# Scaling of attention probabilities on ScalarE instead of VectorE in a two-block transformer kernel on one core

## The reference, cut to what matters

```python
s = jnp.einsum('nibkgd,nijkd->nikgbj', qb, kb).astype(jnp.float32) * (dh ** -0.5) + bias
s = jnp.where(mask[None, :, None, None], s, NEG_INF)
m = jnp.max(s, axis=-1)
if sink is not None:
    sk = sink.astype(jnp.float32).reshape(Hk, G)[:, :, None]
    m = jnp.maximum(m, sk)
p = jnp.exp(s - m[..., None])
denom = jnp.sum(p, axis=-1)
if sink is not None:
    denom = denom + jnp.exp(sk - m)
p = p / denom[..., None]
o = jnp.einsum('nikgbj,nijkd->nibkgd', p.astype(v.dtype), vb)
```

## Time and profile before

| | us |
|---|---|
| three timed runs, median | 3052.56 |
| lowest and highest of them | 3052.38, 3054.38 |
| the profiled execution's own time | 3057.37 |
| its span, first to last instruction | 3055.6 |
| PE busy in the span | 2493.0 (82%) |
| DVE busy | 1438.0 (47%) |
| ACT busy | 862.8 (28%) |
| POOL busy | 686.3 (22%) |
| bytes read from HBM | 1094 MB, 359 GB/s over the span |

### The profile page before, as it was taken

One profiled execution on the slowest core, in us unless ns is written; L12 is line 12 of the kernel. 1 busy time (PEld: TensorE's weight loads), 2 busy tenths in 40 slices (PEclk: granted clock), 3 DMA queues, 4 the chain that ended last, 5 costly groups with the idle time before them and its releaser, 6 DMA issues.

```text
span 3055.6 us, 32772 instructions
## 1 busy us (share of the span) xinstructions
PE 2493.0 (82%) x11448; PEld 1318.3 (43%) x11448; DVE 1438.0 (47%) x3379; ACT 862.8 (28%) x2297; POOL 686.3 (22%) x638
## 2 busy tenths in 40 slices
PE   8999865667999966657898987798987989877777
PEld 7777311113977421213555532264542645422222
DVE  3363100002255201000467667778657786677774
ACT  0231100000122100000233333457434574343343
POOL 4010000002211000000013444424334243444442
PEclk9999978778999987887899999999999999999999
DMA  6337999999434899999716999999999999999997
GB/s 260 137 133 305 424 428 428 428 428 384 166 138 181 371 426 428 427 427 427 310 46 274 422 421 421 421 421 421 415 422 421 416 393 417 420 421 422 421 419 312
DMA packets 121205, 1100.41 MB, mean 360 GB/s; under 512 B 13488, under 2 KB 17360, under 8 KB 21968
## 3 DMA queue, kind: packets, MB, share of 16 engines
q1 hardware_dynamic: 45584, 558.26, 43.9%
q0 software_dynamic: 73728, 536.90, 42.4%
q10 hardware_dynamic: 1728, 3.14, 0.3%
HBM read 1094.06 MB, written 4.19 MB: 359 GB/s over the span
## 4 chain that ended last, share of the span: by engine, by line
DMA 44%; PE 42%; DVE 8%; issue 3%; ACT 3%; POOL 1%; DVEq 0%; SPq 0%; ACTq 0%; POOLq 0%
DMA wbuf<-in_puv,ar 20%; PE ps L711 18%; PE ps L1431 9%; DMA wbuf<-in_w_expert_up 8%; DMA wbuf<-in_w_expert_down 8%; DMA wbuf<-in_w_expert_gate 5%; PE ps L901 4%; PE ps L1080 3%; DVE ar L2240 3%; DMA wbuf<-in_w_mem_kv 2%; PE ps L866 2%; PE ps L715 2%; ACT ar L2303 1%; PE ps L811 1%; PE ps L834 1%
## 5 line engine op out<-in xcount | busy, mean ns | idle before, releaser
L1431 PE MATMUL ps<-wbuf,ar 128*128 128x512 f32 x2048 | 969.4, 612 | 214.8 <-ACT ar L2303 214.4
L2240 DVE CUSTOM_DVE_ANT_0 ar<-wbuf,Y 128x1024 f32<-128x1024 f32 x512 | 628.4, 1227 | 334.5 <-DMA wbuf<-in_puv,ar 325.0
L2862 POOL DMA_INDIRECT wbuf<-in_puv,ar x512 | 554.3, 1083 | 863.7 <-PE ps L1431 745.6
L1431 PEld LDWEIGHTS ps<-wbuf,ar 128*128 128x128 f32 x2048 | 370.0, 193 | 765.1 <-issue 763.2
L1080 PE MATMUL ps<-wbuf,ar 128*32 128x512 f32 x2944 | 458.8, 760 | 284.1 <-DMA wbuf<-in_w_expert_up 113.0
L2303 ACT ACTIVATE ar<-ar 128x1 f32<-128x1 f32 (+1 forms) x1053 | 270.4, 257 | 667.3 <-DVE ar L2240 635.4
L711 PE MATMUL ps<-HT,wbuf 128*128 128x256 f32 (+1 forms) x2304 | 396.7, 331 | 4.9 <-DMA wbuf<-in_w_mem_kv 4.9
L711 PEld LDWEIGHTS ps<-HT,wbuf 128*128 128x128 f32 x2304 | 350.2, 193 | 50.6 <-issue 10.8
L1080 PEld LDWEIGHTS ps<-wbuf,ar 128*32 128x32 f32 x2944 | 93.1, 125 | 632.5 <-issue 212.7
L2300 ACT COPY ar<-ps 128x512 f32<-128x512 f32 (+4 forms) x135 | 70.1, 519 | 700.8 <-PE ps L1080 297.3
L2828 POOL TENSOR_TENSOR sm<-sm,co 128x1 f32<-128x1 f32 (+1 forms) x18 | 10.1, 561 | 1094.6 <-DVE sm L1466 1094.3
(11 more groups left out here) (188 smaller groups left out, 1954.1 us busy)
## 6 DMA issues: line engine op xcount, KB each, us to landing
wbuf<-in_w_expert_down SPq DMA_DIRECT2D x64, 2048.0 KB, 31.3
wbuf<-in_w_expert_up SPq DMA_DIRECT2D x62, 2048.0 KB, 30.9
wbuf<-in_w_expert_gate SPq DMA_DIRECT2D x58, 2048.0 KB, 30.8
wbuf<-in_w_in SPq DMA_DIRECT2D x22, 2048.0 KB, 9.5
wbuf<-in_peer_w_q SPq DMA_DIRECT2D x12, 2048.0 KB, 11.5
wbuf<-in_w_o SPq DMA_DIRECT2D x6, 2048.0 KB, 11.6
wbuf<-in_b_w_in SPq DMA_DIRECT2D x6, 2048.0 KB, 11.4
wbuf<-in_w_branch_b SPq DMA_DIRECT2D x4, 2048.0 KB, 7.5
```

The source lines that it names most:

```text
L1431: m = T.e.matmul(acc[n][:, :], DG[:, j % 4, :], rows_of(name)[:, 1024 + 512 * n:1536 + 512 * n], start=(j == 0), stop=(j == 127))
L2240: V.did(V.e.tensor_tensor_reduce(JK, rows_of(f"g{l}{i}.{j}")[:, 0:1024], Y[:, i, :], 1.0, 0.0, ALU.mult, ALU.add, DT[:, i, j:j + 1]), f"do ...
L2862: G.land(G.e.indirect_dma_start(out=rows_of(name), out_offset=None, in_=I["puv"], in_offset=bass.IndirectOffsetOnAxis(ap=IX[:, i, j:j + 1] ...
```

## The change

Three edits, all in `attend`. On VectorE the copy of the sink columns goes, and for units with a `scale` so does the multiplication; the reciprocal gets a name (`.rc`) so that ScalarE can wait for it. On ScalarE the copy of the sink columns comes ahead of the exponentials of its unit, and after the exponentials of unit k the tile of unit k-1 is multiplied by its reciprocals, as an activation `Copy` with a scale for each partition: one of 128x512 for a dilated unit, two of 128x256 for a windowed one. The other attentions keep their multiplication on VectorE.

```diff
@@ -1575,8 +1575,6 @@
                         u = units[k]
                         if k >= nt:
                             V.wait_ge(*at[f"{p}.t{k - nt}.{4 * ((len(units[k - nt]['blk']) - 1) // 4)}"])
-                        if "sink" in u:
-                            copy(u["tb"][:, 256:514:257], u["sink"])
                         for gi, g in enumerate(u["soft"]):
                             for n, (bi, c0, w, tab, col0) in enumerate(g["parts"]):
                                 V.wait_ge(*at[f"{p}.s{k}.{bi}"])
@@ -1598,8 +1596,8 @@
                     if 0 <= k - 1 < len(units):
                         u = units[k - 1]
                         V.wait_ge(*at[f"{p}.e{k - 1}"])
-                        recip(u["den"], u["den"])
-                        for gi, g in enumerate(u["soft"]):
+                        recip(u["den"], u["den"], *([f"{p}.rc{k - 1}"] if "scale" in u else []))
+                        for gi, g in enumerate(u["soft"] if "scale" not in u else []):
                             a0, n = g["cols"][0], 128 * len(u["blk"]) // len(u["soft"])
                             ts(u["tb"][:, a0:a0 + n], u["tb"][:, a0:a0 + n], g["den"], None, ALU.mult, None,
                                *([f"{p}.n{k - 1}"] if gi + 1 == len(u["soft"]) else []))
@@ -2370,6 +2368,8 @@
                         A.wait_ge(*at[f"{p}.nm{k}"])
                         if k >= nt:
                             A.wait_ge(*at[f"{p}.t{k - nt}.{4 * ((len(units[k - nt]['blk']) - 1) // 4)}"])
+                        if "sink" in u:
+                            copy(u["tb"][:, 256:514:257], u["sink"])
                         for gi, g in enumerate(u["soft"]):
                             a0, n = g["cols"]
                             bi, c0, _, tab, _ = g["parts"][0]
@@ -2380,6 +2380,13 @@
                             else:
                                 act(u["tb"][:, a0:a0 + n], u["tb"][:, a0:a0 + n], ACT.Exp, *names,
                                     bias=g["nm"], scale=u.get("scale", 1.0), accum_out=g["den"])
+                    if 0 <= k - 1 < len(units) and "scale" in units[k - 1]:
+                        u = units[k - 1]
+                        A.wait_ge(*at[f"{p}.rc{k - 1}"])
+                        for gi, g in enumerate(u["soft"]):
+                            a0, n = g["cols"][0], 128 * len(u["blk"]) // len(u["soft"])
+                            act(u["tb"][:, a0:a0 + n], u["tb"][:, a0:a0 + n], ACT.Copy,
+                                *([f"{p}.n{k - 1}"] if gi + 1 == len(u["soft"]) else []), scale=g["den"])
                     j = k - lag
                     if 0 <= j < len(units):
                         u, nb = units[j], len(units[j]["blk"])
```

## The result

The changed kernel takes 3059.39 us in the median of 20 runs (3057.18 to 3063.45), the kernel before 3053.01 us in the median of 20 (3048.93 to 3056.88). The ratio is 1.0023, 95% interval 1.0016 to 1.0029, so the change costs 7.0 us (4.9 to 8.9). The forecast was 3057.0, with 3052 to 3061 as its range: inside, but the mean lies just beyond the 6.1 us that I had called no change, in the class that had got 0.18.

The account below looks back on a forecast made before the run. PE was taken to bound the attention, passing its delays on one for one. Tails 2 x (1.1 + 0.2), stall -0.4, clock +2.7 - 0.5 gave +4.4 us on 3052.56: 3057.0, range 3052.0 to 3061.0.

Parts of the forecast that it names:

- the class that had got 0.18: Outcome that the changed kernel is slower by over 0.2% (6.1 us); chance 0.18.
- Part 1: Steady steps of both attentions: scaling on ScalarE stays covered; net between -0.1 and +0.1 us, taken as 0.
- the 0.6 of cover: Usual windowed step: 0.6 us left between ScalarE's scaled tile (145.31) and PE's request for it (145.91).
- Part 2: Tail of the dilated attention: PE gets unit 7's tile later, +1.1 us a layer, bounds +0.9 and +1.3.
- Part 3: Tail of the windowed attention: PE gets its last scaled tiles later, +0.2 us a layer, bounds 0.1 and 0.5.
- Part 4: Second layer near 892 us: stall of VectorE's scalings beside GpSimd's sums goes, -0.4 us, between -0.47 and 0.
- Part 5: TensorE's clock after dilated tails: new fall in second layer, +2.7 us; less work at half pace in first, -0.5.
- B: Clock does as before in both layers, PE only loses the tails: 3054.8 us; chance 0.28.
- C: Clock falls in both layers, in neither in the timed runs of before: 3060.2 us; chance 0.14.
- E: ScalarE becomes the pace of the windowed steps: 3063 us and more with the tails; chance 0.05.
- F: Multiplying copy between exponentials makes ScalarE reload tables, 1.28 us each, in each step: over 3080 us; chance 0.02.

Follow-up runs that it names:

- late_l0: Kernel before with 120 identity transposes on PE between the first layer's two attentions; 3064.32 against 3052.32 us, ratio 1.0040.
- tails_dve: Changed kernel with the last two units of each attention scaled on VectorE as before; 3050.90 against 3052.82 us for the kernel before, ratio 0.9995.
- win_only: Kernel before with only the windowed attention's scaling and the sink copies moved to ScalarE; 3056.10 against 3052.82 us, ratio 1.0014.
- dil_only: Kernel before with only the dilated attention scaled on ScalarE; 3056.88 against 3052.82 us, ratio 1.0014.
- tail_units: Kernel before with only the last two units of each attention scaled on ScalarE; 3058.23 against 3051.52 us, ratio 1.0021.
- copy_last: Changed kernel with ScalarE's copy of unit 5's transposed tile behind unit 7's scaling in the dilated tails; 3059.32 us, ratio 1.0023 to the kernel before.
- win_tail: Kernel before with only the last two units of the windowed attention scaled on ScalarE; 3052.76 against 3051.52 us, ratio 1.0005.
- sink_only: Kernel before with only the copy of the sink columns moved to ScalarE; 3051.82 against 3052.82 us, ratio 1.0001.
- after_filler: Changed kernel with 12, 3 and 4 unread identity transposes in PE's dilated-tail waits; 3054.47 against 3052.32 us for the kernel before, ratio 1.0009.
- before_filler: Kernel before with 7, 1 and 4 unread identity transposes in PE's dilated-tail waits; 3051.16 against 3052.32 us, ratio 0.9997.

## Why the prediction was right or wrong

**PE bounds the attention and passes its delays on one for one: right,** within the scatter; late_l0 shows it. In the changed kernel's profile 1.35 us of the first layer's shift seem to be gone at the second (491.73 us through the experts against 493.08), but that stretch varies as much among kernels with the same attention.

**Part 1, nothing in the steady steps: right in the whole** (51.83 us in every dilated attention, tails_dve 0.9995), with a hole. I left beside GpSimd's sums only what I saw, VectorE's scalings held up. The negative maximum is a VectorE instruction too, and its delay now goes on through ScalarE, whose chain to the scaled tile is longer. First layer:

```profile
163.63 1.27 POOL L2850 TENSOR_TENSOR wbuf<-wbuf 128x512 f32<-128x512 f32 x1 [98.69 <-DMA wbuf<-in_w_branch_b]
163.75 1.17 DVE L1469 SCALAR_TENSOR_TENSOR sm<-sm 128x2 f32<-128x2 f32 x1
...
166.49 1.05 ACT L2301 ACTIVATE ar<-ar,sm 128x256 f32<-128x256 f32 x2
...
167.60 0.66 PE L715 MATMUL ps<-co,ar 128*128 128x128 f32 x4 [0.24 <-ACT ar L2301]
```

The negative maximum, 0.16 us undisturbed, ends with GpSimd's first sum (164.92 and 164.90). Its 1.17 us use up the 0.6 of cover, and PE loses 0.31 us against its old schedule in this step, and 0.37 and 0.36 in two steps of the second layer. It depends on where the sums fall in the step: tails_dve and win_only, with the same steps, lost nothing in either layer.

**Part 2, dilated tail: right mechanism, size off.** The term was +1.09 us a layer; it is 1.34 and 1.34 (shift of unit 7's transposes, 130.57 to 132.56 in a profile that ran 0.65 late before it; 862.20 to 864.69 with 1.15). The step that failed is "start to start 0.50 of its 0.58" for the copy, and 0.63 before it for the scaling of unit 6. I had read an overlap of 0.1 us from an exponential and the accumulator read behind it. That pair does overlap, other pairs don't: the starts lie 0.75 and 0.62 us apart, duration and 0.03. My upper bound, nothing overlaps, 1.3, was what happened. A row that I had would have told: the copy at 129.76 follows the read of 0.19 us at 129.55 by 0.21, its full duration and more.

**Part 3, windowed tail: mechanism right, size off.** +0.2 expected, 0.55 measured in each layer, above the upper bound of 0.5: the same mistake, 1.05 us for two scalings instead of 0.93. Two more things failed. The gain from the sink copy that I gave unit 14 isn't there: the last read stands as late against PE's work as before (218.00 and 216.02 us, with PE's products starting at 215.24 and 213.28). So unit 14's tile is 0.62 us late, not 0.36. And ahead of unit 15's scalings I had forgotten ACT's copy (219.30, 0.58); they are ready just when PE has done the products before, and PE doesn't wait for unit 15. What remains is unit 14's delay, less 0.07.

**Part 4, the stall that goes: not shown.** VectorE's scalings are no longer held up, but the sums hold up the maximum instead. The Trainium skill (SBUF — State Buffer, section on the two separate sides) says that of VectorE and GpSimd, when both need the port pair that they share, the one that starts second waits out the other's whole instruction, and that ScalarE never waits there. The trace agrees: the negative maximum above ends 0.02 us after GpSimd's sum, and ScalarE's 32 windowed scalings of that layer all take 0.51 us. What it is worth to PE can't be read from the pair of profiles alone, where the changed kernel loses 0.51 us more (stalls of 0.31 and 0.75 us for 0.01 and 0.54): the same steps stall or don't in other profiles. Of the 12 windowed attentions whose steady units ScalarE scales, 6 have stalls, 0.23 us on average over the 12; of the 14 with VectorE 6 have some, 0.28 on average. So one kind of stall has taken the place of the other, with no gain or loss that these can tell: about -0.1 us for both layers, where I had -0.4.

**Part 5, the clock: right way, one size off.** Kernels that scale the dilated tail on ScalarE (changed, dil_only, tail_units, copy_last) fell in 8 tails of 8; those that leave it on VectorE, without filler (before, win_only, win_tail, tails_dve, sink_only, late_l0), in 7 of 12; with filler in 0 of 6. I priced the second layer's new fall at 2.7 us, that of the first layer before. It cost 1.43: the granted clock is 0.50 in 866 to 869 us, but 1.00 again from 869.2 on, at the end of the value products, while in the first layer it is 1.00 only from 138.7 on, when later products have run at the lower level too. A fall costs 1.4 to 2.8 us, 1.95 on average in the 8 tails and 2.17 in six of the 7 (late_l0's first has the added transposes in it). So the change adds 2 x 1.95 - 2 x 7/12 x 2.17 = 1.4 us on average, and 1.1 in the two profiles (2.45 + 1.43 - 2.77), where I had 2.2. That no tail of before was sure to hold or to fall I had only in rivals B and C; its one profile showed one of each, close to its mean.

**The sum.** 2 x 1.34 + 2 x 0.55 - 0.1 + 1.4 = 5.1 us, where I had 2.2 + 0.4 - 0.4 + 2.2 = 4.4; measured are 7.0 (4.9 to 8.9), 6.4 in the medians. That 4.4 comes so near 5.1 is in part luck: the tails were 1.2 us too low and the clock 0.8 too high. Shown are the tails (tail_units, tails_dve) and the clock (after_filler). The traces' 5.1 lies at the lower end of the interval; what makes the rest, if it isn't scatter, isn't shown. One candidate is left: nobody sees the falls of the timed executions. If the kernel before falls less often in them than in 7 of 12, the clock term grows, up to 3.9 for none. before_filler's gain of 0.9 us, where the profiles' falls would give 2.5, would fit that, but its interval (-3.7 to 1.8 us) settles nothing.

**Rivals.** C has the changed kernel right (a fall in both layers) and, as far as the profiles show, the kernel before wrong. E (ScalarE as the pace) and F (table loads) are out: PE waits only in the tails and beside the sums, and the table loads are 106 in both profiles. The Trainium skill (ScalarE: Activation LUTs, rules for kernel authors) says to use VectorE, not ScalarE, for multiplications. Here that comes out right for the last units, where each instruction's latency counts (tail_units 1.0021), and makes no difference that can be measured for the other 20 of 24 a layer (tails_dve 0.9995).

**Open.** win_only took 3.3 us more in the median, and its trace accounts for about 1; the changed kernel took 7.0, and the traces account for about 5. And the profiles can't say why a tail with the old waits falls in one execution and not in another.

## What to carry to other kernels

Before moving a step off an engine that isn't the bound, look at where its chain is bare: in a pipelined loop the last units have no side work behind them, and there a slower instruction, a further hop and a foreign copy in the queue count nearly in full. Move the steady units and leave the last ones on the faster engine. Where TensorE must wait in pieces just before dense work, cheap transposes in the wait can keep its clock; and a queue's instructions should be added up start to start from pairs of the same kind. A stall of half a microsecond that one profile shows may be missing from the next one of the same steps: before a term is put on it, count it in several.

## What the runs showed of the hardware that I had not expected

Activations on ScalarE don't overlap here: 0.75 us from start to start for one of 0.72, 0.62 for a copy of 0.59, 1.05 us for two of 0.51. Only an accumulator read starts before its activation ends, 0.63 us after a start of 0.72 (129.56 to 130.19 in the changed kernel). Successive transposes of a tile or of the identity start 0.11 us apart at full clock (12 in 1.47 us, of which the last one's 0.27), and 0.21 while the granted clock was 0.50, as the first eight of late_l0's 120. A fall of the clock has no fixed price: 1.4 to 2.8 us for the same list of products, by how many of them ran before the clock was back.
